# A decoder step's output product and feed-forward start from operands split one program ahead, and the last down products take three inner blocks of a pair, then the fourth

## The chip, the core and the metric

One core of a Trainium2 chip runs the whole program. The metric is the device time of one execution in microseconds (us). The engines are TensorE (PE in the profile; PEld is its weight load), VectorE (DVE), ScalarE (ACT), GpSimd (POOL) and SyncE (SP), which here only issues DMAs.

## What is computed

One inference step of one decoder layer, for a prompt of 1024 positions and 32 sample positions, all in float32. The part that matters here is the end of the layer:

```
gate = sigmoid(proj[..., OFF_MG:OFF_MG + 3 * D_MODEL].reshape(bn, t, 3, D_MODEL))
h = gate[:, :, 0] * (o_a @ wa) + gate[:, :, 1] * (o_b @ wb) + gate[:, :, 2] * (o_c @ wc)
x = x + h @ wo
...
q = rms_norm((rms_norm(x, g_x) @ w_q).reshape(bn, t, M_HEADS, M_HD), q_g)
...
x = x + o @ w_o
h = jnp.square(jax.nn.relu(rms_norm(x, g_f) @ w1))
return x + h @ w2
```

D_MODEL is 1024, the feed-forward's hidden width is 4096, and the attention between runs over 256 memory tokens with 4 heads of 128.

## The kernel before

Activations lie with channels on the 128 partitions: `x`, `h` and the like are 8 blocks (KD = 8) of 128 channels by T = 1056 positions. A product over all positions is made in three chunks (NC3 = 3) of NW = 352 positions. Every operand of the large products is split in two fp32r parts: ScalarE copies it rounded (the high part), VectorE subtracts that from the original (the low part), and TensorE adds high x high, high x low and low x high into one PSUM bank. A product of one 128-column weight block with one chunk is thus 8 x 3 = 24 matmuls.

The program is a row of stages, each a block with one instruction list for each engine. At the end of a block all engines meet in a barrier; within it they wait for each other by semaphores. The order on an engine is the order in which the code is written. Four stages matter here.

`stage_merge` (L2937) goes through 24 units: for each branch and each of 8 output blocks, gate product (TensorE, L2983 to L2985), sigmoid (ScalarE, L3032), branch product (L2994 to L2996), and VectorE's multiply and add into `h` (L3065, L3068). Weight blocks of a unit arrive by SP's DMAs into two buffers in turn.

`stage_merged_query` (L3078) makes x + h @ w_out and then, from the normed x, the memory queries. Its 12 weight blocks (8 of `w_out`, 4 of `w_mq`) go through three raw buffers `mw_raw` (NRAW = 3), loaded by SP; a later one is requested when VectorE has made the low part of the block three ahead (L3103 to L3106). `weight_high` (L3156) and `weight_low` (L3207) split them into `mw_slots`. ScalarE and VectorE start this stage with

```
merged_high(0)                 # ScalarE
weight_high(0)
...
merged_low(0)                  # VectorE
weight_low(0)
```

where `merged_high(c)` and `merged_low(c)` split a third of `h` (8 blocks of 352 positions, 2816 elements in a partition) into `h_h` and `h_l`. TensorE waits for both, then runs chunk 0 of all eight blocks, then chunks 1 and 2. GpSimd brings the thirds of x back from memory.

`stage_mem` (L3454) is the memory attention and its output product. At its end it norms x for the feed-forward, for positions 0 to 383 and 384 to 767 ("the middle"): squares, sums by TensorE, root, inverse, `scaled` (L3895) into `xf_scaled`, then the split into `xf_h` and `xf_l`. SP requests the first three blocks of `w_ff1` into `ff_raw` when the attention's last values are there. The middle is only scaled here and split in the next stage.

`stage_ffn` (L3286) has 64 units, each with one weight block of 128 x 1024 elements. An up unit makes one of 32 hidden blocks (relu, square, high part by ScalarE, low part by VectorE, into a ring of five). A down unit takes four hidden blocks (GB = 4; 8 groups, NG = 8) into two output blocks (z = 0, 1), for three chunks each: 72 matmuls (L3386 to L3388). The PSUM banks go in two sets of three in turn; `bank_free(n)` waits until the set's last content was read. The last group's down units come behind the last up unit. Ahead of its 72 matmuls a down unit waits with `e.wait_ge(s_hl, GB * (g + 1))` for all four hidden blocks. The stage opens with weight block 0's split, TensorE's `chunk(0, 0)`, the sums of squares for positions 768 on, `chunk(1, 0)`, the middle's chunks and then the end's.

Of the kernel before, what the change touches and what calls it, by code (L numbers as in the profile page):

```python
# [28 lines left out]
P = 128  # L29
# [502 lines left out]
def raw_slots(nc, K, ctx, tag, kb, nraw):  # L532

    R = Shared()
    R.nraw, R.at = nraw, nc.sbuf_base
# [2401 lines left out]
def stage_merge(nc, K, h, xh, xl, oh, lows, first):  # L2937
# [6 lines left out]
    with ctx:  # L2944
# [16 lines left out]
        def _(e):  # L2961
            for u in range(NU):
# [8 lines left out]
                e.dma_start(braw[:, u % 2, :, :], K.d[names[br]][0, :, P * m:P * m + P].rearrange("(k p) n -> p k n", p=P)).then_inc(s_bin[u % 2], 16)  # L2971

# [27 lines left out]
        def _(e):  # L3000
# [25 lines left out]
            for u in range(NU):  # L3026
# [10 lines left out]
                if u + 2 < NU:  # L3037
                    gate_high(u + 2)

# [38 lines left out]
def stage_merged_query(nc, K, w, wq, h, hh, hl, x, q, h_at, free_at):  # L3078
# [3 lines left out]
    raw = nc.alloc_sbuf_tensor_at("mw_raw", [P, NRAW, KD, P], F32, offset=free_at)  # L3082
    near = nc.alloc_sbuf_tensor_at("mw_slots", [P, 6, 2, KD, P], F32R, offset=free_at + NRAW * KD * P * 4)
# [4 lines left out]
    with nc.Block() as block:  # L3088
        s_hh, s_hl, s_x = K.sem("mw_merged_high"), K.sem("mw_merged_low"), K.sems("mw_x_in", NC3)
        s_in, s_wh, s_wl = K.sems("mw_weights_in", NRAW), K.sem("mw_weights_high"), K.sem("mw_weights_low")  # L3090
# [26 lines left out]
        def _(e):  # L3117
# [34 lines left out]
        def _(e):  # L3152
# [3 lines left out]
            def weight_high(j):  # L3156
                e.wait_ge(s_in[j % NRAW], 16 * (j // NRAW + 1))
                if j in (6, 7):
                    e.wait_ge(s_hl, NC3)
# [4 lines left out]
            def squares(c):  # L3164
                e.wait_ge(s_out, count(c, KD - 1))
                e.wait_ge(s_hl, NC3)
# [13 lines left out]
            merged_high(0)  # L3180
            weight_high(0)
# [20 lines left out]
        def _(e):  # L3202
# [4 lines left out]
            def weight_low(j):  # L3207
                e.wait_ge(s_wh, j + 1)
# [31 lines left out]
            merged_low(0)  # L3240
            weight_low(0)
            weight_low(1)
# [43 lines left out]
def stage_ffn(nc, K, xh, xl, xl32, x, ahead):  # L3286
# [20 lines left out]
    with ctx:  # L3307
        W = weight_slots(nc, K, ctx, "ff", KD, ahead=ahead)
        hh = ctx.enter_context(nc.sbuf_tensor("ff_hidden_high", [P, RING, T], F32R))
        hl = ctx.enter_context(nc.sbuf_tensor("ff_hidden_low", [P, RING, T], F32R))  # L3310
        act = ctx.enter_context(nc.sbuf_tensor("ff_act", [P, 2, T], F32))
        rstd = ctx.enter_context(nc.sbuf_tensor("ff_rstd", [P, T - LAST], F32))
# [5 lines left out]
        s_mid_h, s_mid_l = K.sem("ff_middle_high"), K.sem("ff_middle_low")  # L3318
# [19 lines left out]
        def _(e):  # L3338
# [12 lines left out]

            e.wait_ge(W.s_lo, 1)
# [7 lines left out]
            e.wait_ge(s_mid_h, 1)  # L3360
            e.wait_ge(s_mid_l, 1)
# [8 lines left out]
            for u, un in list(enumerate(units))[2:]:  # L3370
# [7 lines left out]
                g = un[1]  # L3378
                e.wait_ge(s_hl, GB * (g + 1))
                for z in range(2):  # L3380
                    bank_free(n)
                    for c in range(NC3):
                        o, ns = K.ps[:, 3 * (n % 2) + c, 0:NW], slice(NW * c, NW * c + NW)
                        for k in range(GB):
                            r = (GB * g + k) % RING
                            e.matmul(o, W.hi[:, u % NSPL, 2 * k + z, :], hh[:, r, ns], start=k == 0, stop=False)  # L3386
                            e.matmul(o, W.hi[:, u % NSPL, 2 * k + z, :], hl[:, r, ns], start=False, stop=False)  # L3387
                            mm = e.matmul(o, W.lo[:, u % NSPL, 2 * k + z, :], hh[:, r, ns], start=False, stop=k == GB - 1)  # L3388
                    mm.then_inc(W.s_mm, 1)
# [33 lines left out]
        def _(e):  # L3423
            low_block(e, W, 0)
            low_block(e, W, 1)
            e.wait_ge(s_mid_h, 1)
# [797 lines left out]
```

## Time and profile before

| what | us |
|---|---|
| median of 3 timed runs | 3068.53 (3067.25 to 3068.81) |
| the profiled execution's own time | 3066.65 |
| its span in the trace | 3064.4 |
| TensorE busy with matmuls | 2743.6 (90%) |
| VectorE busy | 1156.6 (38%) |
| ScalarE busy | 795.6 (26%) |

The span is what the trace covers; the execution's time has 2.2 us more around it. TensorE's busy time is the sum over its matmuls, which overlap one another; its clock has two levels, and the profile gives the granted one as a share of the full clock (0.50 or 1.00 in a stretch that lies wholly at one level). A timeline row gives the start, the duration, the engine, the line, the output and the inputs, and in brackets how long the engine had been idle and what ended it.

### The profile page before, as it was taken

The page shows a single profiled execution, that of the slowest core. Times are in us where ns is not written, and L with a number is a line of the kernel's source. Part 1 is how long each engine was busy: PE and PEld are TensorE (multiplying, and loading weights), DVE is VectorE, ACT ScalarE, POOL GpSimd, SP SyncE. Part 2 cuts the span into 40 slices and gives each one's busy share as a digit, 9 for nine tenths or more (in the row PEclk, how much of TensorE's full clock was granted, in tenths as well). Part 3 has the DMA queues.
Part 4 walks back from the last instruction along what each step waited for, and adds up shares of the span by engine and source line. Part 5 has one row for each costly group of instructions (what it writes and reads, how often), then busy time and mean ns, then how long its engine had stood idle before and what let it go on. Part 6 is the DMA issues. An engine that isn't in the chain of part 4 may idle for free. (4 is left out here: it accounts for less than half of the span.)

```text
span 3064.4 us, 49130 instructions
## 1 busy us (share of the span) xinstructions
PE 2743.6 (90%) x21538; PEld 2451.1 (80%) x21538; DVE 1156.6 (38%) x2018; ACT 795.6 (26%) x1243; POOL 163.6 (5%) x215
## 2 busy tenths in 40 slices
PE   5898688886997789988899999899889999999998
PEld 4897588863995555544699999898679999999998
DVE  4433644425053556534222232443443222222222
ACT  3223322211114244432222121221433221222221
POOL 1000222201111000012000000000000000000000
PEclk7999799987998799988899999998999999999999
DMA  4610100004430000047511111401311111111111
GB/s 163 233 50 8 16 3 3 3 4 161 99 85 18 3 1 1 1 142 264 210 52 45 48 46 43 139 10 35 117 28 42 49 42 49 49 48 43 49 42 64
DMA packets 178933, 192.09 MB, mean 63 GB/s; under 512 B 18214, under 2 KB 162897, under 8 KB 173624
## 3 DMA queue, kind: packets, MB, share of 16 engines
q1 hardware_dynamic: 168665, 127.05, 14.0%
q0 software_dynamic: 9888, 61.87, 5.8%
q8 instruction: 170, 2.79, 0.4%
q14 instruction: 42, 0.34, 0.0%
q10 hardware_dynamic: 168, 0.04, 0.0%
HBM read 165.28 MB, written 28.00 MB: 63 GB/s over the span
## 5 line engine op out<-in xcount | busy, mean ns | idle before, releaser
L3386 PE MATMUL ps<-ff_hidden_high,ff_high 128*128 128x352 f32 x768 | 249.1, 324 | 4.8 <-issue 4.8
L3387 PE MATMUL ps<-ff_hidden_low,ff_high 128*128 128x352 f32 x768 | 248.9, 324 | 0.0
L3388 PE MATMUL ps<-ff_hidden_high,ff_low 128*128 128x352 f32 x768 | 248.8, 324 | 0.0
L586 PE MATMUL ps<-xf_h,ff_high 128*128 128x352 f32 x720 | 232.3, 323 | 2.0 <-DVE ff_low L575 2.0
L588 PE MATMUL ps<-xf_h,ff_low 128*128 128x352 f32 x720 | 231.1, 321 | 0.0
L587 PE MATMUL ps<-xf_l,ff_high 128*128 128x352 f32 x720 | 230.9, 321 | 0.0
L2983 PE MATMUL ps<-xn_h,me_gate_w_high 128*128 128x352 f32 x576 | 186.6, 324 | 4.9 <-DVE me_gate_w_low L3044 4.9
L2984 PE MATMUL ps<-xn_l,me_gate_w_high 128*128 128x352 f32 x576 | 185.3, 322 | 0.0
L2985 PE MATMUL ps<-xn_h,me_gate_w_low 128*128 128x352 f32 x576 | 185.2, 322 | 0.0
L3448 DVE TENSOR_TENSOR x<-x,ps 128x1056 f32<-128x1056 f32 x64 | 80.3, 1255 | 235.8 <-PE ps L3388 235.7
L3442 DVE TENSOR_TENSOR ff_hidden_low<-ff_act,ff_hidden_high 128x1056 fp32r<-128x1056 f32 x32 | 40.3, 1258 | 307.7 <-ACT ff_hidden_high L3418 307.7
L3386 PEld LDWEIGHTS ps<-ff_hidden_high,ff_high 128*128 128x128 f32 x768 | 145.3, 189 | 5.1 <-issue 5.1
L3396 ACT ACTIVATE ff_high<-ff_raw 128x1024 fp32r<-128x1024 f32 x64 | 67.4, 1053 | 307.6 <-PE ps L3388 297.8
L3388 PEld LDWEIGHTS ps<-ff_hidden_high,ff_low 128*128 128x128 f32 x768 | 145.5, 189 | 0.0
L3387 PEld LDWEIGHTS ps<-ff_hidden_low,ff_high 128*128 128x128 f32 x768 | 145.3, 189 | 0.0
L2164 PE MATMUL ps<-np_probsT,values_ones 128*65 128x512 f32 x264 | 141.9, 621 | 0.0
L586 PEld LDWEIGHTS ps<-xf_h,ff_high 128*128 128x128 f32 x720 | 135.1, 188 | 2.3 <-DVE ff_low L575 2.3
L587 PEld LDWEIGHTS ps<-xf_l,ff_high 128*128 128x128 f32 x720 | 135.4, 188 | 0.0
L588 PEld LDWEIGHTS ps<-xf_h,ff_low 128*128 128x128 f32 x720 | 135.1, 188 | 0.0
L586 PE MATMUL ps<-xn_h,pj_high 128*128 128x352 f32 x336 | 110.4, 329 | 7.6 <-DVE pj_low L575 7.6
L2983 PEld LDWEIGHTS ps<-xn_h,me_gate_w_high 128*128 128x128 f32 x576 | 108.7, 189 | 5.1 <-issue 5.1
L588 PE MATMUL ps<-xn_h,pj_low 128*128 128x352 f32 x336 | 109.6, 326 | 0.0
(686 smaller groups left out, 6447.9 us busy)
## 6 DMA issues: line engine op xcount, KB each, us to landing
ff_raw<-in_w_ff SPq DMA_DIRECT2D x64, 512.0 KB, 4.0
me_gate_w_raw<-in_w_in SPq DMA_DIRECT2D x23, 512.0 KB, 3.9
pj_raw<-in_w_in SPq DMA_DIRECT2D x13, 512.0 KB, 4.4
xn_high<-xn_h POOLq DMA_DIRECT2D x1, 4224.0 KB, 12.1
xn_low<-xn_l POOLq DMA_DIRECT2D x1, 4224.0 KB, 24.1
xn_h<-xn_high POOLq DMA_DIRECT2D x1, 4224.0 KB, 16.0
xn_l<-xn_low POOLq DMA_DIRECT2D x1, 4224.0 KB, 26.4
xn_h<-xn_high SPq DMA_DIRECT2D x1, 4224.0 KB, 13.0
```

The costliest lines, as they stand in the source:

```text
L586: e.matmul(o, W.hi[:, z, k, :], rh[:, k, n], start=k == ks[0], stop=False)
L587: e.matmul(o, W.hi[:, z, k, :], rl[:, k, n], start=False, stop=False)
L588: mm = e.matmul(o, W.lo[:, z, k, :], rh[:, k, n], start=False, stop=k == ks[-1])
L2164: e.matmul(K.ps[0:65, 2 + z, :], va[:, z, j, g, :], PT[:, G % NPT, :], start=first, stop=j == i).then_inc(s_val, 1)
L2983: e.matmul(K.ps[:, c, 0:NW], wh[:, z, k, :], xh[:, k, chunk(c)], start=k == 0, stop=False)
L2984: e.matmul(K.ps[:, c, 0:NW], wh[:, z, k, :], xl[:, k, chunk(c)], start=False, stop=False)
L2985: mm = e.matmul(K.ps[:, c, 0:NW], wl[:, z, k, :], xh[:, k, chunk(c)], start=False, stop=k == KD - 1)
L3386: e.matmul(o, W.hi[:, u % NSPL, 2 * k + z, :], hh[:, r, ns], start=k == 0, stop=False)
L3387: e.matmul(o, W.hi[:, u % NSPL, 2 * k + z, :], hl[:, r, ns], start=False, stop=False)
L3388: mm = e.matmul(o, W.lo[:, u % NSPL, 2 * k + z, :], hh[:, r, ns], start=False, stop=k == GB - 1)
L3396: e.activation(W.hi[:, u % NSPL, :, :], W.raw[:, u % NRAW, :, :], ACT.Copy).then_inc(W.s_hi, 1)
L3448: e.tensor_tensor(c3(x[:, m, :]), c3(x[:, m, :]), bank(n), ALU.add).then_inc(s_read_down, 1)
```

## The change

The raw weight buffers, the weight slots and the first semaphores of the output product are now made ahead of `stage_merge` and handed to it as `soon`. SP requests w_out's blocks 0, 2 and 1 at the merge's end, each when the merge's buffer under it is free. ScalarE copies seven of the eight high blocks of h's first third there, ahead of the last unit's sigmoids, and block 0's high part behind them. The new function `first_product` makes product 0 of chunk 0 in the order high x high, low weights, low h. Likewise `stage_mem` splits the feed-forward's weight block 0, and its last `scaled(1, 4)` is done at the head of `stage_ffn`, where the middle's split now goes in two halves. To make room, `ff_low`, `ff_hidden_low` and two small tiles lie at other addresses. In the last group, the first down unit (q = 0) runs three of the four hidden blocks for both z, then the fourth for both.

```diff
@@ stage_merge, SyncE
+            for j, gates in ((0, NU - 1), (2, NU - 1), (1, NU)):
+                e.wait_ge(s_g, NC3 * gates)
+                e.dma_start(soon.raw[:, j, :, :], soon.w(j).rearrange("(k p) n -> p k n", p=P)).then_inc(soon.s_in[j], 16)
@@ stage_merge, ScalarE
+                if u == NU - 2:
+                    e.wait_ge(s_h, NC3 * (NU - 1))
+                    e.activation(soon.hh[:, 0:KD - 1, 0:NW], h[:, 0:KD - 1, 0:NW], ACT.Copy)
+            e.wait_ge(soon.s_in[0], 16)
+            e.activation(soon.near[:, 0, 0, :, :], soon.raw[:, 0, :, :], ACT.Copy)
@@ stage_merged_query, SyncE
-            for j in range(NB):
-                if j >= NRAW:
-                    e.wait_ge(s_wl, j - NRAW + 1)
+            for j in range(NRAW, NB):
+                e.wait_ge(s_wl, j - NRAW + 1)
@@ stage_merged_query, TensorE
+            def first_product():
+                for k in range(KD):
+                    if k == KD - 1:
+                        e.wait_ge(s_hh, 1)
+                    e.matmul(bank(0), slot(0)[:, 0, k, :], hh[:, k, chunk(0)], start=k == 0, stop=False)
+                e.wait_ge(s_wl, 1)
+                for k in range(KD):
+                    e.matmul(bank(0), slot(0)[:, 1, k, :], hh[:, k, chunk(0)], start=False, stop=False)
+                for k in range(KD):
+                    if k % 4 == 0:
+                        e.wait_ge(s_hl0, k // 4 + 1)
+                    mm = e.matmul(bank(0), slot(0)[:, 0, k, :], hl[:, k, chunk(0)], start=False, stop=k == KD - 1)
+                mm.then_inc(s_mm, 1)
+
+            first_product()
             for c in range(NC3):
-                e.wait_ge(s_hl, c + 1)
+                if c:
+                    e.wait_ge(s_hl, c)
                 for m in range(KD):
+                    if c == 0 and m == 0:
+                        continue
@@ stage_merged_query, ScalarE
-            merged_high(0)
-            weight_high(0)
+            e.activation(hh[:, KD - 1, chunk(0)], h[:, KD - 1, chunk(0)], ACT.Copy).then_inc(s_hh, 1)
             weight_high(1)
@@ stage_ffn, TensorE
+            def down(u, g, z, n, ks):
...
                 g = un[1]
+                if g == NG - 1 and un[2] == 0:
+                    e.wait_ge(s_hl, GB * (g + 1) - 1)
+                    bank_free(n)
+                    down(u, g, 0, n, range(GB - 1))
+                    bank_free(n + 1)
+                    down(u, g, 1, n + 1, range(GB - 1))
+                    e.wait_ge(s_hl, GB * (g + 1))
+                    down(u, g, 0, n, range(GB - 1, GB)).then_inc(W.s_mm, 1)
+                    down(u, g, 1, n + 1, range(GB - 1, GB)).then_inc(W.s_mm, 1)
+                    n += 2
+                    continue
                 e.wait_ge(s_hl, GB * (g + 1))
@@ stage_ffn, ScalarE
-            weights_high(e, 0)
+            weights_high(e, 1)
             e.activation(xl32[:, :, end], x[:, :, end], ACT.Square).then_inc(s_sq, 1)
-            weights_high(e, 1)
-            e.activation(xh[:, :, middle], xl32[:, :, middle], ACT.Copy).then_inc(s_mid_h, 1)
+            e.activation(xh[:, 0:4, middle], xl32[:, 0:4, middle], ACT.Copy).then_inc(s_mid_h, 1)
+            e.wait_ge(s_mid_n, 1)
+            e.activation(xh[:, 4:8, middle], xl32[:, 4:8, middle], ACT.Copy).then_inc(s_mid_h, 1)
@@ stage_mem, ScalarE, behind its last root
+            high_block(e, ahead, 0, 1)
```

VectorE's lists show the rest of it. At the start of the output product VectorE ran this before; `h_l` is the low part of h, `mw_slots` the weight blocks:

```order
L3201 UNCONDITIONAL_BRANCH
L3205 TENSOR_TENSOR h_l<-h,h_h 128x8x352
L3209 TENSOR_TENSOR mw_slots<-mw_raw,mw_slots 128x1024 x2
L3205 TENSOR_TENSOR h_l<-h,h_h 128x8x352
L3209 TENSOR_TENSOR mw_slots<-mw_raw,mw_slots 128x1024
L3205 TENSOR_TENSOR h_l<-h,h_h 128x8x352
L3209 TENSOR_TENSOR mw_slots<-mw_raw,mw_slots 128x1024
L3215 TENSOR_TENSOR x<-x,ps 128x352
```

And now, at the same place:

```order
L3225 UNCONDITIONAL_BRANCH
L3234 TENSOR_TENSOR mw_slots<-mw_raw,mw_slots 128x1024
L3269 TENSOR_TENSOR h_l<-h,h_h 128x4x352 x2
L3234 TENSOR_TENSOR mw_slots<-mw_raw,mw_slots 128x1024
L3229 TENSOR_TENSOR h_l<-h,h_h 128x8x352
L3234 TENSOR_TENSOR mw_slots<-mw_raw,mw_slots 128x1024
L3229 TENSOR_TENSOR h_l<-h,h_h 128x8x352
L3234 TENSOR_TENSOR mw_slots<-mw_raw,mw_slots 128x1024
L3240 TENSOR_TENSOR x<-x,ps 128x352
```

The low part of weight block 0 has moved ahead of h's first low part, which is made in two halves; the work up to block 3 is the same in sum.

At the end of the memory attention and the start of the feed-forward VectorE ran this before:

```order
L3892 RECIPROCAL mm_rstd<-mm_rstd 128x384
L3884 TENSOR_TENSOR x<-x,ps 128x288
L3897 SCALAR_TENSOR_TENSOR xf_scaled<-x,par,mm_rstd 128x384 x4
L3884 TENSOR_TENSOR x<-x,ps 128x288 x3
L3897 SCALAR_TENSOR_TENSOR xf_scaled<-x,par,mm_rstd 128x384 x4
L3472 UNCONDITIONAL_BRANCH
L3422 UNCONDITIONAL_BRANCH
L575 TENSOR_TENSOR ff_low<-ff_raw,ff_high 128x1024 x2
L3427 TENSOR_TENSOR xf_l<-xf_scaled,xf_h 128x8x384
L3429 TENSOR_SCALAR ff_rstd<-ps 128x288
```

And now:

```order
L3940 RECIPROCAL mm_rstd<-mm_rstd 128x384
L3932 TENSOR_TENSOR x<-x,ps 128x288
L575 TENSOR_TENSOR ff_low<-ff_raw,ff_high 128x1024
L3945 SCALAR_TENSOR_TENSOR xf_scaled<-x,par,mm_rstd 128x384 x4
L3932 TENSOR_TENSOR x<-x,ps 128x288 x3
L3519 UNCONDITIONAL_BRANCH
L3465 UNCONDITIONAL_BRANCH
L3468 SCALAR_TENSOR_TENSOR xf_scaled<-x,par,mm_rstd 128x384 x4
L575 TENSOR_TENSOR ff_low<-ff_raw,ff_high 128x1024
L3474 TENSOR_TENSOR xf_l<-xf_scaled,xf_h 128x4x384 x2
L3476 TENSOR_SCALAR ff_rstd<-ps 128x288
```

One weight split has crossed the stage's end (the two branch rows) upwards, and one scaling downwards.

## Rows read from the trace of the kernel before

**Rows 1.** The page's first part: busy time of each engine, its share, instructions

```profile
PE 2743.6 (90%) x21538; PEld 2451.1 (80%) x21538; DVE 1156.6 (38%) x2018; ACT 795.6 (26%) x1243; POOL 163.6 (5%) x215
```

**Rows 2.** Timeline from the merge to the output product: start, duration (us), engine, line, out<-in

```profile
1947.92 0.47 ACT L3032 ACTIVATE me_gate_sigmoid<-ps 128x352 f32<-128x352 f32 x1 [3.35 <-PE ps L2985]
...
1953.29 0.32 PE L2996 MATMUL ps<-merge_operand_high,me_branch_w_low 128*128 128x352 f32 x1
...
1954.31 0.53 DVE L3068 TENSOR_TENSOR h<-h,me_gate_sigmoid 128x352 f32<-128x352 f32 x1
...
1957.72 3.09 DVE L3205 TENSOR_TENSOR h_l<-h,h_h 128x2816 fp32r<-128x2816 f32 x1 [2.88 <-ACT h_h L3154]
...
1960.73 1.22 DVE L3209 TENSOR_TENSOR mw_slots<-mw_raw,mw_slots 128x1024 fp32r<-128x1024 f32 x1
...
1962.09 0.63 PE L3123 MATMUL ps<-h_h,mw_slots 128*128 128x352 f32 x1 [8.48 <-DVE mw_slots L3209]
...
1974.99 1.22 DVE L3209 TENSOR_TENSOR mw_slots<-mw_raw,mw_slots 128x1024 fp32r<-128x1024 f32 x1
...
1976.26 0.43 PE L3123 MATMUL ps<-h_h,mw_slots 128*128 128x352 f32 x1
```

**Rows 3.** Timeline from the memory attention's end into the feed-forward

```profile
2288.32 1.38 DVE L3884 TENSOR_TENSOR x<-x,ps 128x288 f32<-128x288 f32 x3
...
2288.91 0.29 PE L3599 MATMUL ps<-mm_o_high,mm_w_low 128*128 128x288 f32 x1
...
2289.61 2.20 DVE L3897 SCALAR_TENSOR_TENSOR xf_scaled<-x,par,mm_rstd 128x384 f32<-128x384 f32 x4
...
2294.57 0.66 PE L3347 MATMUL ps<-xf_h,ff_high 128*128 128x352 f32 x1 [5.37 <-DVE ff_low L575]
...
2299.82 4.04 PE L3356 MATMUL ps<-xf_scaled,cst 128*128 128x288 f32 x16
...
2303.89 0.46 DVE L3429 TENSOR_SCALAR ff_rstd<-ps 128x288 f32<-128x288 f32 x1 [1.62 <-PE ps L3356]
...
2312.65 2.56 DVE L3437 TENSOR_TENSOR xf_l<-xf_scaled,xf_h 128x2304 fp32r<-128x2304 f32 x1 [2.23 <-ACT xf_h L3407]
```

**Rows 4.** Timeline around the start of the last group's down units

```profile
2988.20 1.22 DVE L575 TENSOR_TENSOR ff_low<-ff_raw,ff_high 128x1024 fp32r<-128x1024 f32 x1
...
2994.70 0.32 PE L588 MATMUL ps<-xf_h,ff_low 128*128 128x352 f32 x1
...
2995.06 1.05 ACT L3414 ACTIVATE ff_act<-ps 128x1056 f32<-128x1056 f32 x1 [7.12 <-PE ps L588]
...
2998.45 1.26 DVE L3442 TENSOR_TENSOR ff_hidden_low<-ff_act,ff_hidden_high 128x1056 fp32r<-128x1056 f32 x1 [9.04 <-ACT ff_hidden_high L3418]
...
2999.81 0.63 PE L3386 MATMUL ps<-ff_hidden_high,ff_high 128*128 128x352 f32 x1 [4.79 <-issue]
```

**Rows 5.** Table of stretches: length; busy us (instructions) by engine; granted clock, DMA share, GB/s

```profile
1962.10:1966.30 4.20, 4.20 (x14) 4.20 (x15) 0.91 (x1) 2.00 (x2) 0.00 (x0) 0.50 1.10 321
...
2294.60:2297.40 2.80, 2.80 (x10) 2.80 (x11) 1.15 (x1) 2.80 (x3) 0.00 (x0) 0.50 0.50 136
2335.00:2994.00 659.00, 659.00 (x4113) 659.00 (x4112) 171.39 (x142) 150.89 (x144) 0.00 (x0) 1.00 0.15 46
2999.80:3004.00 4.20, 4.19 (x14) 4.20 (x15) 1.05 (x1) 0.00 (x0) 0.00 (x0) 0.50 0.02 4
```

**Rows 6.** Timeline at the boundary from the feed-forward to the store stage

```profile
3047.91 0.32 PE L3388 MATMUL ps<-ff_hidden_high,ff_low 128*128 128x352 f32 x1
...
3048.26 1.25 DVE L3448 TENSOR_TENSOR x<-x,ps 128x1056 f32<-128x1056 f32 x1 [4.50 <-PE ps L3388]
...
3049.84 0.41 PE L4017 MATMUL ps<-cst,x 128*128 128x128 f32 x2 [1.61 <-PEq L3307]
```

**Rows 7.** All DMAs into `mw_raw`, from issue to landing

```profile
DMA to landing us min/median/max: 3.8/6.8/11.7
```

**Rows 8.** Timeline: the feed-forward's third unit, behind a short wait

```profile
2325.36 0.43 PE L586 MATMUL ps<-xf_h,ff_high 128*128 128x352 f32 x1 [2.04 <-DVE ff_low L575]
```

More of the change, by code:

```diff
@@ L2934, in _, with stage_merge @@
             to_channels(1)
[L2937 removed]
+def stage_merge(nc, K, h, xh, xl, oh, lows, first, soon):
     names = ("w_br_a", "w_br_b", "w_br_c")
@@ L3238, in norm_low @@
                 e.tensor_tensor(hl[:, :, chunk(c)], sq[:, :, :], hh[:, :, chunk(c)].bitcast(F32), ALU.subtract).then_inc(s_xl, 1)
-            merged_low(0)
             weight_low(0)
+            e.wait_ge(s_hh, 1)
+            for z in range(2):
+                ks = slice(4 * z, 4 * z + 4)
+                e.tensor_tensor(hl[:, ks, chunk(0)], h[:, ks, chunk(0)], hh[:, ks, chunk(0)].bitcast(F32), ALU.subtract).then_inc(s_hl0, 1)
             weight_low(1)
@@ L3283, in _, with stage_ffn @@
                 take(2, m)
-def stage_ffn(nc, K, xh, xl, xl32, x, ahead):
+def stage_ffn(nc, K, xh, xl, xl32, x, ahead, at):
     GB = 4
@@ L3317, in stage_ffn @@
             "squared", "summed", "mean", "root", "normed", "high", "low"))
-        s_mid_h, s_mid_l = K.sem("ff_middle_high"), K.sem("ff_middle_low")
+        s_mid_n, s_mid_h, s_mid_l = (K.sem("ff_middle_" + x) for x in ("normed", "high", "low"))
         c3 = lambda ap: ap.rearrange("p (c n) -> p c n", c=NC3)
@@ L3350, in chunk @@
                 return mm
+            def down(u, g, z, n, ks):
+                for c in range(NC3):
+                    o, ns = K.ps[:, 3 * (n % 2) + c, 0:NW], slice(NW * c, NW * c + NW)
+                    for k in ks:
+                        r = (GB * g + k) % RING
+                        e.matmul(o, W.hi[:, u % NSPL, 2 * k + z, :], hh[:, r, ns], start=k == 0, stop=False)
+                        e.matmul(o, W.hi[:, u % NSPL, 2 * k + z, :], hl[:, r, ns], start=False, stop=False)
+                        mm = e.matmul(o, W.lo[:, u % NSPL, 2 * k + z, :], hh[:, r, ns], start=False, stop=k == GB - 1)
+                return mm
             e.wait_ge(W.s_lo, 1)
@@ L3381, in _ @@
                     bank_free(n)
[L3382 to L3389, printed above, removed]
+                    down(u, g, z, n, range(GB)).then_inc(W.s_mm, 1)
                     n += 1
@@ L3423, in _ @@
         def _(e):
-            low_block(e, W, 0)
+            for k in range(4, KD):
+                mm = e.scalar_tensor_tensor(xl32[:, k, middle], x[:, k, middle], K.p("norm_ffn_g", k), ahead.rstd[:, 1, :], ALU.mult, ALU.mult)
+            mm.then_inc(s_mid_n, 1)
             low_block(e, W, 1)
-            e.wait_ge(s_mid_h, 1)
-            e.tensor_tensor(xl[:, :, middle], xl32[:, :, middle], xh[:, :, middle].bitcast(F32), ALU.subtract).then_inc(s_mid_l, 1)
+            for z in range(2):
+                ks = slice(4 * z, 4 * z + 4)
+                e.wait_ge(s_mid_h, z + 1)
+                e.tensor_tensor(xl[:, ks, middle], xl32[:, ks, middle], xh[:, ks, middle].bitcast(F32), ALU.subtract).then_inc(s_mid_l, 1)
             e.wait_ge(s_sum, 1)
@@ L3995, in _ @@
                 if m == 4:
+                    low_block(e, ahead, 0)
                     scaled(1, 0)
-            scaled(1, 4)
 def stage_store(nc, K, x):
```

46 lines of the change are left out of this document (28 added, 18 removed).

## Prediction

> **What bounds the kernel now.** I read the page first for the busy shares: TensorE has by far the most work, 2743.6 us of matmuls in a span of 3064.4 us, so the time falls where TensorE idles or runs at its lower clock [rows 1]. The change touches three places, and at each I read the timeline for what TensorE waits for, then the table of stretches for the clock that was granted.
>
> Place A, from the merge of the branches to the output product [rows 2]: TensorE's last merge matmul is issued at 1953.29. VectorE ends the last unit at 1954.31 + 0.53 = 1954.84; behind the block boundary ScalarE makes the high parts of h's first third and of the first weight block, VectorE's two subtractions follow, and TensorE's first matmul comes at 1962.09. It was idle for 8.48 us.
>
> Place B, from the memory attention to the feed-forward [rows 3]: last matmul issued at 2288.91, VectorE still scales until 2289.61 + 2.20 = 2291.81, then ScalarE and VectorE split weight block 0, and TensorE starts at 2294.57, having idled for 5.37 us.
>
> Place C, ahead of the last four down units [rows 4]: the last up matmul is issued at 2994.70, its hidden block is ready (high and low part) at 2998.45 + 1.26 = 2999.71, TensorE goes on at 2999.81. The row calls the 4.79 us of idle time "issue", but the 0.10 us between that subtraction's end and the matmul show what it waited for.
>
> Behind each of these waits the table grants 0.50, the lower of the two levels (1.2 GHz): 14 matmuls in 4.2 us at A and C, 10 in 2.8 us at B [rows 5]. That is 0.30 us for a matmul. At full clock (2.4 GHz) it is 659 us / 4113 = 0.160 us [rows 5]. So each such matmul costs 0.14 us extra: 2.0 us at A and C, 1.4 us at B.
>
> **The change at A.** Blocks 0 to 2 of the output weights are loaded during the merge, block 0's high part and seven of the eight high blocks of h's first third are made there, and the first product takes all high x high, then low weights, then low h. TensorE no longer needs anything from the new block for its first seven matmuls. The boundary costs 0.33 us from VectorE's last end to TensorE's first start, as before the store stage (3048.26 + 1.25 = 3049.51 to 3049.84) [rows 6]. So TensorE starts at 1954.84 + 0.33 = 1955.17.
>
> That is not the gain yet: behind it VectorE has to keep up. Its list up to block 3's low part is now: low block 0 (1.22), half and half of the first h_l (1.62 each, between 1.26 for 1056 elements and 3.09 for 2816), low block 1 (1.22), h_l (3.09), low block 2 (1.22), h_l (3.09), low block 3 (1.22) [rows 2, 4]. Sum 14.30; each of the 7 steps starts 0.08 us before the one ahead has ended (1957.72 + 3.09 against 1960.73), so 13.7 us, and block 3 is ready at 1955.17 + 13.7 = 1968.9. TensorE could be there a little earlier: a product is 24 x 0.16 = 3.84 us, and it meets low block 1 at 1960.7, low block 2 at 1964.8 and low block 3 at 1968.9, with some 0.3 us of waiting at each. Before, block 3 was ready at 1974.99 + 1.22 = 1976.21 and held TensorE up just so, until 1976.26 [rows 2]. **Gain 1976.2 - 1968.9 = 7.3 us.** The clock drops out of this term: even with 14 matmuls at 0.30 us the first product is over at 1955.17 + 4.2 + 1.6 = 1961.0, and three products of 3.84 us bring TensorE to block 3 at 1968.7, still ahead of VectorE.
>
> What was moved, queue by queue: SP issues three of the weight DMAs behind its last merge DMA, where it had nothing left to do; block 1's waits for the last gate product, which ScalarE's sigmoid answers at 1947.92 [rows 2], and has 7.3 us until the boundary, where these DMAs take 3.8 to 11.7 us, median 6.8 [rows 7]; ScalarE asks for it first at about 1955.7 and VectorE at 1959.4. ScalarE's copy of seven blocks (2464 elements, under the 2.55 us of 2816) stands ahead of the last unit's sigmoids. VectorE wants these only when the branch product ends, some 9 us later, so it costs nothing. Blocks 3 to 7 are requested when a low block is done, so all requests come some 7 us earlier together with what needs them. The first of them, block 3, is asked for at 1956.4 with the first third of x in flight: at the median it lands at 1963.2, at the longest landing at 1968.1. The latter makes low block 3 ready at 1968.1 + 1.06 + 1.22 = 1970.4 and leaves 5.8 us. Above, the bound is 7.6 (no wait of 0.3). I take 7.3, since the row itself is of the same chain; bounds 5.8 to 7.6.
>
> **The change at B.** Weight block 0 is split inside the attention stage: ScalarE's copy of 1.06 us lies behind its last root, where it has nothing left in that stage; VectorE's 1.22 us subtraction goes in ahead of the last scaling, and one scaling of 2.20 us goes out to the new stage. VectorE's last addition thus ends at 2288.32 + 1.38 + 1.14 = 2290.84 instead of the scaling at 2291.81, and TensorE starts at 2291.17 [rows 3]. The additions pushed back are not waited for: TensorE's last product needs a bank freed by an addition that stays ahead of the new subtraction.
>
> From there: first chunk 24 x 0.16 = 3.84, then the sums of squares, from whose start to VectorE's mean it is 2303.89 - 2299.82 = 4.07 us [rows 3]. That frees the chain mean, root, inverse, scaling, high, low, from VectorE's 2303.89 to 2312.65 + 2.56 = 2315.21, that is 11.32 us [rows 3]; TensorE reaches it a little early (three more chunks are 11.5 us). So the mean starts at 2291.17 + 3.84 + 4.07 = 2299.08. The moved work must be done by then: scaling to 2293.4, low block 1 to 2294.5, the middle third's copies in two halves behind the square to about 2297.0, their subtractions to 2299.0. Just in time; if late by a few tenths, the gain falls by that. **Gain 2303.89 - 2299.1 = 4.8 us.** At the lower clock it would be 4.8 - 1.4 = 3.4.
>
> Which clock? TensorE's idle time shrinks from 5.37 us to 2291.17 - 2289.20 = 2.0 us. The nearest row is the matmul at 2325.36, with 2.04 us of idle time before it: it takes 0.43 us [rows 8], where the first ones behind the long waits take 0.63, 0.66 and 0.63 [rows 2 to 4]. No fall there. I take the full clock; bounds 3.4 to 4.9.
>
> The Trainium skill, page "TensorE: Matmul & The Clock Gate", section "Part 1: The HAM clock gate", says that the gate is opened by sustained activity and closed by idleness, and that its monitor runs free of the kernel, so that the point varies from run to run. By that rule a gap of this length may still be met by a closing gate in some executions, and the sum at B would be 3.4 instead of 4.8; the 2.04 us gap of this trace didn't meet one.
>
> **The change at C.** The last hidden block isn't needed for three quarters of the first down unit. Two column blocks x 3 chunks x 3 inner blocks x 3 = 54 matmuls now run first, 54 x 0.16 = 8.6 us from 2994.86, over at 3003.5; the hidden block is ready at 2999.71 [rows 4]. Their weights were ready at 2988.20 + 1.22 = 2989.42 [rows 4], and the second bank is free when ScalarE's first activation has read it, about 2996.1, needed at 2999.2. So the wait of 2999.81 - 2994.86 = 4.95 us goes, and with no idle time the fall of the clock too, 2.0 us. What is new: both halves of the unit now end together, 9 matmuls apart. The next unit's first half needs the first half's bank: VectorE's addition starts 0.35 us after the last matmul's issue and takes 1.25 (3047.91 to 3048.26) [rows 6], 1.6 us in all, where TensorE has 10 x 0.16 = 1.6 us of work. A wait of about 0.1 us. **Gain 6.95 - 0.1 = 6.85 us**; bounds 6.4 (the wait 0.5 us) to 7.0.
>
> **Sum.** 7.3 + 4.8 + 6.85 = 18.95 us of the profiled execution: span 3064.4 to 3045.5, its time 3066.65 to 3047.7. The median of the three timed runs, 3068.53, lies 1.9 above that execution, so the forecast is 3068.5 - 18.95 = 3049.6. The bounds add up to 15.6 to 19.5.
>
> **Rivals.** (1) Late weights in the output product. For it: up to 11.7 us to land, and in the shown stretch the DMA share is 1.10 where the first matmuls run [rows 5, 7]. Against: each request moves with its user. The gain at A falls to 5.8, or less when later blocks are late too (2 to 3 us more): 3051 to 3054, 10%. (2) The lower clock at B (with it perhaps 0.3 us of waits): 3051, 12%. (3) The head starts are eaten at the boundary: some engine comes through later than 0.33 us, or a moved split stands in another's way, so that A and B give half and C all: 6 + 6.85 = 13, 3055.5, 5%. (4) Slower. Place: the feed-forward's opening. It now meets TensorE after a short idle with no long wait; if the gate stays at 0.50 there and does not open for a long stretch, each matmul costs 0.14 us. 18.95 / 0.14 = 135 matmuls eat the gain, 180 make the kernel slower by 6 us; 300 of them (the first four up units) cost 42 us: 3092. Against it: behind every long wait the level is back after 10 to 14 matmuls, and 4113 matmuls from 2335 to 2994 run at 1.00 [rows 5]. 3%. (5) The same time within 0.2% (6.1 us, about what a measurement of this kernel can tell from no change) would need two of the three places to fail: 4%.
>
> **How the numbers follow.** The forecast with its bounds has 66%, (1) and (2) together 22, (3) 5, (4) 3, (5) 4. Forecast, (1), (2) and (3) are all faster by over 6.1 us: 93%. Low end: the largest gain from the lowest time shown, 3066.65 - 19.5 = 3047, less 1 us for the spread of runs; high end: to rival (3), 3056.
>
> **What would show it.** A: TensorE's first output matmul 0.3 to 0.4 us behind VectorE's last merge row, low block 3 about 13.7 us behind it. B: under 2.3 us of idle time, granted clock 1.00 in the first chunk, the mean 8 us behind the start. C: no gap ahead of the down units, no stretch at 0.50, a wait of 0.1 us after the 72nd matmul. A first matmul at A later than 1956.5, 0.50 at B, or a gap of over 0.5 us behind C's first unit would prove the terms wrong.

## The result and the profile after

| | before | after |
|---|---|---|
| first comparison, median us (range, executions) | 3068.67 (3067.25 to 3071.55, 4) | 3040.94 (3039.11 to 3043.73, 4) |
| the same two kernels again | 3068.74 (3059.91 to 3079.71, 17) | 3043.53 (3041.49 to 3046.99, 6) |
| ratio after to before, first and again (95% interval) | | 0.9906 [0.9895, 0.9918]; 0.9916 [0.9899, 0.9933] |
| span of the first profiled execution | 3064.4 | 3036.9 |

The change makes the kernel 25 to 28 us faster; 18.95 were forecast, and 3040.94 lies below the range given (3046 to 3056). The direction was right, the size too small by 6 to 9 us.

Place A after the change, timeline (start, duration, engine, line, output and inputs, idle time before):

```profile
1947.85 0.53 DVE L3076 TENSOR_TENSOR h<-h,me_gate_sigmoid 128x352 f32<-128x352 f32 x1
...
1948.70 1.53 PE L3145 MATMUL ps<-h_h,mw_slots 128*128 128x352 f32 x8 [1.55 <-PEq L2944]
1948.70 1.23 DVE L3234 TENSOR_TENSOR mw_slots<-mw_raw,mw_slots 128x1024 fp32r<-128x1024 f32 x1 [0.32 <-PEq L2944]
...
1954.18 0.43 PE L3130 MATMUL ps<-h_h,mw_slots 128*128 128x352 f32 x1 [0.22 <-DVE mw_slots L3234]
...
1958.18 1.06 ACT L3187 ACTIVATE mw_slots<-mw_raw 128x1024 fp32r<-128x1024 f32 x1 [2.22 <-DMA mw_raw<-in_w_out]
...
1961.19 1.22 DVE L3234 TENSOR_TENSOR mw_slots<-mw_raw,mw_slots 128x1024 fp32r<-128x1024 f32 x1
...
1962.46 0.43 PE L3130 MATMUL ps<-h_h,mw_slots 128*128 128x352 f32 x1
```

The 8.48 us of idle time of [rows 2] are 1.55. TensorE starts 0.32 us behind VectorE's last merge row (1948.38); low block 3 is ready at 1962.41, 13.7 us later, and TensorE takes it up at 1962.46. ScalarE does wait for a DMA at 1958.18, but VectorE is busy with h_l until 1961.26 meanwhile.

Place B after, timeline:

```profile
2275.53 1.22 DVE L575 TENSOR_TENSOR ff_low<-ff_raw,ff_high 128x1024 fp32r<-128x1024 f32 x1
...
2278.78 1.18 DVE L3932 TENSOR_TENSOR x<-x,ps 128x288 f32<-128x288 f32 x3
...
2280.27 0.40 PE L3376 MATMUL ps<-xf_h,ff_high 128*128 128x352 f32 x1 [1.75 <-PEq L3519]
...
2284.17 4.04 PE L3395 MATMUL ps<-xf_scaled,cst 128*128 128x288 f32 x16
...
2288.25 0.46 DVE L3476 TENSOR_SCALAR ff_rstd<-ps 128x288 f32<-128x288 f32 x1
```

The idle time ahead of the feed-forward is 1.75 us in place of 5.37 [rows 3], the first matmul takes 0.40 us, not 0.66, and VectorE's mean comes 7.98 us behind it.

Place C after, timeline:

```profile
2974.19 0.32 PE L588 MATMUL ps<-xf_h,ff_low 128*128 128x352 f32 x1
2974.35 0.32 PE L3386 MATMUL ps<-ff_hidden_high,ff_high 128*128 128x352 f32 x1
...
2977.96 1.26 DVE L3489 TENSOR_TENSOR ff_hidden_low<-ff_act,ff_hidden_high 128x1056 fp32r<-128x1056 f32 x1 [9.05 <-ACT ff_hidden_high L3461]
...
2985.68 0.32 PE L3388 MATMUL ps<-ff_hidden_high,ff_low 128*128 128x352 f32 x1
2986.01 0.40 PE L3386 MATMUL ps<-ff_hidden_high,ff_high 128*128 128x352 f32 x1
```

The gap of 4.79 us [rows 4] is gone. The hidden block is ready at 2979.22, while TensorE is still at the three older ones. The new wait for a bank is the step from 2985.68 to 2986.01, 0.33 us in place of 0.16.

Table of stretches after (length; busy us and instructions of PE, PEld, DVE, ACT, POOL; granted clock, DMA share, GB/s): the same 4113 matmuls as [rows 5]'s long stretch, the first 24 feed-forward matmuls (B), the start of the output product (A), and a piece of the last down units (C).

```profile
2319.50:2973.57 654.07, 654.07 (x4113) 654.07 (x4113) 170.95 (x142) 150.82 (x144) 0.00 (x0) 1.00 0.16 47
2280.30:2284.10 3.80, 3.80 (x24) 3.80 (x25) 3.31 (x5) 3.80 (x3) 0.00 (x0) 1.00 0.49 142
1948.70:1953.00 4.30, 3.73 (x20) 3.13 (x20) 4.30 (x4) 4.30 (x4) 0.96 (x1) 1.00 0.44 126
2979.00:2983.00 4.00, 4.00 (x27) 4.00 (x27) 1.35 (x2) 0.00 (x0) 0.00 (x0) 1.00 0.00 0
```

The clock is full at all three places now. The first row is the surprise: 4113 matmuls at full clock in 654.07 us, where [rows 5] has 659.00 for as many, with TensorE busy without a gap in both. No instruction was taken out of this stretch.

### The profile page after: what moved, and what is told of

It is laid out like the page before. It is cut to its first block and busy times, and to the rows that moved or that the text cites. A ratio compares the mean times of both kernels' runs of the same rounds, so it can differ in the third digit from the quotient of the medians.

```text
span 3036.9 us, 49131 instructions
## 1 busy us (share of the span) xinstructions
PE 2730.9 (90%) x21538; PEld 2440.2 (80%) x21538; DVE 1156.6 (38%) x2020; ACT 795.2 (26%) x1245; POOL 163.7 (5%) x215
```

## Where 27.5 us of span went

I cut both spans at the first matmul of each stage.

| stretch | before | after | less |
|---|---|---|---|
| start to the merge's first matmul (none of it changed) | 1539.4 | 1532.8 | 6.6 |
| merge and output product (A) | 583.2 | 576.2 | 7.0 |
| memory attention (its end holds half of B) | 172.0 | 171.4 | 0.6 |
| feed-forward (rest of B, C) | 755.3 | 742.0 | 13.3 |

The three terms I had priced come to 19.0 of it: A 7.0; C 7.0, from the last up matmul to the store stage; and B 5.0, from the memory attention's last matmul to VectorE's mean (14.98 us before, 10.02 after). The rest, some 8.5 us, is 4.9 us in the feed-forward's 4113 matmuls, 6.6 us in stages that the change doesn't touch, and 2.9 us the other way: from its first to its last matmul the memory attention took 166.4 us before and 169.3 after. (That was the first profile's luck and not the change: before profiled again has 169.6 there, and over all 14 profiles two have 166.4 and 166.6 and twelve 169.1 to 170.1.) Two theories had to be tested: that the 4.9 us come from **where the tiles lie** (the change moves five of the feed-forward's to make room: beside ff_low, ff_hidden_low and the small ff_rstd also ff_hidden_high and ff_act, which the description of the change doesn't list), and that the rest is **the lower clock coming at other moments** in each execution, so that two single profiles differ by it whatever the code. The rival to the second was that the change itself shortens the early stages.

## Experiments

### One part alone, and one part undone

Third part alone (the kernel before, with the branch of the change's last diff piece in stage_ffn):

```diff
+                if g == NG - 1 and un[2] == 0:
+                    e.wait_ge(s_hl, GB * (g + 1) - 1)
...
+                    down(u, g, 0, n, range(GB - 1, GB)).then_inc(W.s_mm, 1)
+                    down(u, g, 1, n + 1, range(GB - 1, GB)).then_inc(W.s_mm, 1)
```

> The kernel before with the third part of the change alone (the last group's first down unit takes three hidden blocks for both z, then the fourth). My term C says 6.85 us less than before (6.4 to 7.0): the 4.95 us of idle time ahead of the last down units gone, no stretch at 0.50 behind it, about 0.1 us of new waiting. In the comparison of the two traces this place gave 7.1 us. Rival: the three parts are not independent and this one alone gives less than 6 or more than 8 us. A second reading rides on it: everything ahead of the last group is the code of before, at the addresses of before, so by both theories of the extra 8.6 us (placement of tiles; luck of the clock) the mean step from one matmul to the next in the down units stays at 161.2 to 161.4 ns, but by the luck of the clock the untouched attention stages may come out anywhere between before's and after's length (nsa prompt stage 349.7 to 353.1 us, sample stage 189.1 to 192.8 us).

Measured: 3062.97 us (12 executions) beside 3068.34 for before (25), ratio 0.9981 [0.9973, 0.9990], so 5.4 us less; below the 6.4 to 7.1 by the medians, within their interval. In its profile the gap is gone and no stretch behind it is at 0.50. Its feed-forward takes 750.7 us, where before profiled again takes 756.9: 6.2 us less. How many matmuls run at 0.50 behind the gap isn't fixed: 11 in before again, 14 in [rows 5], 17 in the next kernel and in every other one that has the moved tiles and not this part, so that the part is worth more there.

Third part undone in the changed kernel (diff as above, with the signs turned):

> The changed kernel with the last group's down units as before (the third part undone). By term C it is 6.4 to 7.1 us longer than the changed kernel, that is some 20.5 to 21.3 us shorter than before; the idle stretch of 4.8 us ahead of the last down units and 14 matmuls at 0.50 are back, and the down units' step stays at 158.3 to 160.5 ns. If the step went with the split down unit instead of with the tiles' place, it is back at 161.3 ns and the kernel is 11 to 12 us longer than the changed one.

Measured: 3052.16 us (5 executions), 0.9946 [0.9933, 0.9959], 16.2 below before, where 20.5 to 21.3 were expected: that rested on the 27.7 us of the first comparison. From the changed kernel's 3043.53 it is 8.6 us away. The gap is back, to the digit, and the clock behind it (timeline, then table of stretches, of this kernel):

```profile
2982.02 0.63 PE L3424 MATMUL ps<-ff_hidden_high,ff_high 128*128 128x352 f32 x1 [4.79 <-issue]
```

```profile
2981.10:2985.30 4.20, 3.28 (x11) 3.31 (x12) 1.95 (x2) 0.47 (x1) 0.00 (x0) 0.50 0.01 4
```

Its feed-forward takes 749.1 us where the changed kernel has 742.0: 7.1 for C in place. The 4113 matmuls take 654.07 us here as well, so the shorter steps don't hang on the split down unit.

First part alone (stage_mem, stage_ffn and the feed-forward's tiles as in before; the merge and output product as in after):

> The kernel before with the first part alone (the output product's operands are split in the merge). Term A says 7.3 us less (5.8 to 7.6); the comparison of traces gave 7.1. If the clock's luck upstream is in fact tied to this part (its code stands ahead of nothing that runs before the merge's end, but the three stages in front came out 6.6 us shorter in the changed kernel), the gain is 13 to 14 us, and the prompt and sample attention stages come out at 349.7 and 189.1 us; if it is not tied, they come out as in before (353.1 and 192.8) or mixed, and the median gain stays at 7.

Measured: 3059.89 us (7 executions), 0.9978 [0.9966, 0.9991], 8.5 less by the medians; the interval, 2.8 to 10.4, holds the 7.3. Merge and output product take 575.5 us in this profile against 583.2, which is 7.7. Upstream the prompt stage took 355.1 us and the sample stage 190.7, neither before's pair nor after's: not tied to this part.

Second part alone, with the placement that it needs:

> The kernel before with the second part alone (feed-forward weight block 0 split in the memory attention, one scaling moved behind it), with the placement that it needs. Term B says 4.8 us (3.4 with the lower clock in the first chunk), the placement 4.9: together 8.3 to 9.7 us below before. TensorE's gap ahead of the feed-forward is 2.0 us. By the clock gate's free running this gap, in this other history, may meet a fall: then the first ten or so matmuls take 0.29 us each and B gives 3.4. If the parts are no sum of their own (the rival), the gain is under 5 or over 13 us.

Measured: 3057.43 us (12 executions), 0.9963 [0.9950, 0.9976], 11.3 less, where 8.3 to 9.7 were expected. By the medians the three parts alone, 8.5, 11.3 and 5.4, come to 25.2 us. The opening is that of the changed kernel, to the digit:

```profile
2294.60 0.40 PE L3348 MATMUL ps<-xf_h,ff_high 128*128 128x352 f32 x1 [1.75 <-PEq L3487]
```

### The same kernels again

> The changed kernel as it is, timed and profiled again beside the kernel before. In the runs so far the kernel before ranges over 11.6 us (3062.8 to 3074.4), its median 3068.3; the undone parts give 5.4 (third part alone), 8.5 (first part alone), 1.9 (placement alone) and 16.2 us (all but the third), which don't add up to 27.7. Theory 'parts plus placement': the three parts (7.1, 4.9, 7.1) and the placed tiles (4.9) make 24 us, the rest of the first comparison was the luck of the clock in few runs; the median is 3043 to 3046 (22 to 26 us below before), and the stages that the change doesn't touch come out differently from profile to profile (merge starting anywhere between 1532 and 1540 us). Rival 'the clock is the change's doing': the stages ahead of the merge get shorter in every execution of the changed kernel; the median stays at 27 to 28 us below before, the merge starts at 1532 to 1534 and the time at 0.50 ahead of it is 337 to 340 us again.

> The kernel before as it is, one more profile. By 'luck' the time at 0.50 ahead of the merge lies anywhere between 337 and 351 us (the six profiles so far, in kernels whose code is the same up to there: 351, 337, 342, 350, 340, 338), and the short wait in the feed-forward's third unit, which met no fall of the clock in the first profile (first matmul 0.43 us), may meet one here. By 'the change's doing' it is 350 us again. The down units' step is 161.2, 161.3 and 161.4 ns again by either.

Measured: after 3043.53 us, 25.2 below before's 3068.74; before again 3063.79 in its one execution. The untouched stages, by the table of stretches (prompt attention, then sample attention), first before:

```profile
993.50:1346.60 353.10, 308.99 (x1384) 190.80 (x1385) 191.85 (x650) 135.35 (x249) 0.00 (x0) 0.91 0.01 3
1346.60:1539.40 192.80, 154.30 (x853) 95.53 (x853) 73.70 (x175) 48.29 (x85) 30.02 (x31) 0.84 0.68 247
```

before again:

```profile
993.30:1343.10 349.80, 305.81 (x1385) 189.66 (x1385) 191.70 (x651) 135.33 (x249) 0.00 (x0) 0.92 0.01 3
1343.10:1532.50 189.40, 152.32 (x852) 94.50 (x853) 73.60 (x175) 48.16 (x85) 29.59 (x31) 0.85 0.70 251
```

and after again:

```profile
995.40:1348.20 352.80, 309.23 (x1385) 191.40 (x1386) 191.80 (x651) 135.43 (x249) 0.00 (x0) 0.91 0.01 3
1348.20:1540.50 192.30, 152.71 (x853) 94.51 (x853) 73.60 (x175) 48.18 (x85) 29.58 (x31) 0.84 0.69 247
```

VectorE's and ScalarE's busy times agree to 0.2 us; what differs is the granted clock, 0.91 or 0.92 and 0.84 or 0.85. The short stages belong to before the second time and the long ones to after: the rival falls, and the 6.6 us were the luck of two single executions. Over all 14 profiles the prompt stage ranges from 349.7 to 355.2 us and the sample stage from 188.6 to 196.6, with no order by kernel.

The same holds at a place I had used as evidence. The short wait of [rows 8] in before again, timeline:

```profile
2321.30 0.66 PE L586 MATMUL ps<-xf_h,ff_high 128*128 128x352 f32 x1 [2.04 <-DVE ff_low L575]
```

The same 2.04 us of idle time, but 0.66 us for the matmul, not 0.43: here the clock fell, for 11 matmuls. It fell at this wait in the profiles of before again, of the first and the third part alone and of all three kernels with only tiles moved; that it didn't in the first profile was the exception, one in seven. In those six the opening was dearer as well, 13 matmuls at 0.50 and not 10, as the table of stretches of the first part alone shows:

```profile
2286.30:2290.10 3.80, 3.80 (x13) 3.80 (x14) 1.22 (x1) 3.80 (x3) 0.00 (x0) 0.50 0.49 142
```

With part B the opening is at full clock in all seven profiles, behind 1.75 us of idle time. The third unit's wait is still there, and the clock stayed full in six of the seven (after, first profile):

```profile
2309.72 0.43 PE L586 MATMUL ps<-xf_h,ff_high 128*128 128x352 f32 x1 [2.05 <-DVE ff_low L575]
```

In the seventh, with the hidden tiles on multiples of 128 bytes, it fell six matmuls later, for 12 of them. So this wait (2.04 to 2.09 us) is followed by 0.50 in six of seven executions whose opening was at 0.50, and in one of seven where the opening was not. That the two hang together is what the counts say; why, the runs don't show.

### Where the tiles lie

Addresses of the feed-forward's tiles, in bytes within a partition:

| tile | before | after |
|---|---|---|
| ff_high | 142304 | 142304 |
| ff_low | 150496 | 180192 |
| ff_hidden_high | 158688 | 150496 |
| ff_hidden_low | 179808 | 188384 |
| ff_act | 200928 | 171616 |

All of them (and ff_rstd, which TensorE doesn't read) at after's places, every instruction as before:

```diff
+        W = weight_slots(nc, K, ctx, "ff", KD, ahead=ahead, low_at=at + 50176)
...
+        hl = nc.alloc_sbuf_tensor_at("ff_hidden_low", [P, RING, T], F32R, offset=at + 58368)
```

> The kernel before with every instruction in its place; only the addresses of the feed-forward's tiles are those of the changed kernel (ff_low and ff_hidden_low behind the others, ff_hidden_high and ff_act closer). Theory 'placement': the 4.9 us by which the feed-forward's inside got shorter, unexplained by the three parts, come from where the tiles lie: the mean step from matmul to matmul in the down units falls from 161.2-161.4 to 158.3-160.5 ns and the kernel is 4 to 5.5 us shorter than before. Rival 'order': the tiles' place does nothing, the steps are shorter since something else runs beside them (or the trace of before was an unlucky one): difference below 1 us, step unchanged at 161.3 ns.

Measured: 3066.43 us (11 executions), 1.9 below before, ratio 0.9991 [0.9982, 1.0000]: less than the 4 to 5.5 expected by the median, and the interval holds both 0 and 5. The timing alone doesn't show the effect; the trace is sharper here, since the steps repeat. The stretch of 4113 matmuls, table of stretches:

```profile
2340.82:2994.85 654.03, 654.03 (x4113) 654.03 (x4112) 170.95 (x142) 150.79 (x144) 0.00 (x0) 1.00 0.16 47
```

Then, in the kernel before, only ff_hidden_low, ff_act and ff_rstd were moved, the hidden low tile to where after has it. (This kernel and the three others of this section that were executed once took 3061.33, 3063.66, 3051.63 and 3046.62 us, in their order.)

> The kernel before with only ff_hidden_low and ff_act placed elsewhere (ff_hidden_low where the changed kernel has it, ff_act ahead of it; ff_hidden_high and ff_low, and so all weight tiles, stay). If the shorter step comes from where ff_hidden_low lies, the step behind the high x low matmuls falls from 161.3 to about 158.9 ns and the other two stay (gain 1.8 us in 768); if it comes from ff_low and ff_hidden_high, all three stay at 161.2 to 161.4. One look is enough, since this step came out within 0.1 ns in every profile of one placement.

```profile
2334.71:2988.75 654.04, 654.04 (x4114) 654.04 (x4113) 170.96 (x142) 150.78 (x144) 0.00 (x0) 1.00 0.15 47
```

My expectation was wrong: not one of the three steps fell but all three. Next, a move of 384 bytes in the kernel before (ff_act and ff_rstd, behind it, move along; shortened):

```diff
-        hl = ctx.enter_context(nc.sbuf_tensor("ff_hidden_low", [P, RING, T], F32R))
+        hl = nc.alloc_sbuf_tensor_at("ff_hidden_low", [P, RING, T], F32R, offset=ahead.at + 49792 + 384)
```

> The kernel before with ff_hidden_low (and ff_act and ff_rstd behind it) 384 bytes higher, all else in place. In the run with only ff_hidden_low and ff_act moved all three steps of the down units came out as in the changed kernel (160.5, 159.0, 158.3 ns), the same for each ring slot and chunk within 0.2 ns, though ff_hidden_high lay 8192 bytes away from where the changed kernel has it. The old and the new address of ff_hidden_low differ by 8576 = 8192 + 384 bytes. Theory 'low address bits': only the 384 count; this kernel has the short steps too (160.5, 158.9, 158.3). Rival 'which neighbour': it was ff_act's place or the tiles' order; the steps stay at 161.2, 161.3, 161.4 ns.

```profile
2337.05:2991.09 654.04, 654.04 (x4114) 654.04 (x4113) 170.97 (x142) 150.81 (x144) 0.00 (x0) 1.00 0.15 47
```

Moving the tile by 384 bytes gives the kernel before the shorter steps. And 128 bytes (with ff_rstd behind it) take them from the changed kernel:

```diff
-        hl = nc.alloc_sbuf_tensor_at("ff_hidden_low", [P, RING, T], F32R, offset=at + 58368)
+        hl = nc.alloc_sbuf_tensor_at("ff_hidden_low", [P, RING, T], F32R, offset=at + 58496)
```

> The changed kernel with ff_hidden_low 128 bytes higher. By 'low address bits' the steps of the down units change again, up to between 158.3 and 161.4 ns or below; the change can't be given beforehand, only that at least one of the three means moves by over 0.5 ns, where from profile to profile of one placement they moved by 0.1. By the rival (only order and neighbours count) they stay at 160.5, 158.9, 158.3.

```profile
2326.63:2985.69 659.06, 659.06 (x4114) 659.06 (x4113) 171.37 (x142) 150.84 (x144) 0.00 (x0) 1.00 0.15 46
```

That is before's stretch again, and its feed-forward takes 747.2 us where after has 742.0. The last two look at 256 bytes more, and at all hidden tiles 32 bytes higher:

> The changed kernel with ff_hidden_low 256 bytes higher. So far the down units' steps came out in two patterns over ring slots and chunks and no third: one where ff_hidden_low starts 96 bytes over a multiple of 512 (kernel before; changed kernel + 128 bytes), with means 161.2, 161.3, 161.4 ns, and one where it starts 480 over (changed kernel; before + 384 bytes), with 160.5, 158.9, 158.3. Here it starts 224 over one, which no kernel had. If the address within 512 bytes sets the step, a third pattern appears; if every placement but the two seen is between them, the feed-forward lasts 742 to 747 us and the kernel 3043 to 3048. A shorter step than 158.9 on average (over 0.5 ns, 1.2 us in 2304) would make this the fastest version. The rest of the kernel is that of the changed one, so it also gives a profile more of the stages that nothing touches.

```profile
2329.69:2983.73 654.04, 654.04 (x4114) 654.04 (x4113) 170.99 (x142) 150.80 (x144) 0.00 (x0) 1.00 0.16 47
```

> The changed kernel with ff_hidden_high, ff_act and ff_hidden_low 32 bytes higher, so that every block of both hidden tiles starts at a multiple of 128 bytes (it was 96 over one). If a read that starts inside a 128-byte piece costs an extra one, the moving operand's 1408 bytes are read in fewer pieces and all three steps fall, to 157 ns or below: up to 1.5 ns x 2304 = 3.5 us. If only the distance between the two tiles counts, nothing changes (160.5, 158.9, 158.3).

```profile
2324.11:2980.93 656.82, 656.82 (x4113) 656.82 (x4113) 171.17 (x142) 150.83 (x144) 0.00 (x0) 1.00 0.16 46
```

With 256 bytes more nothing changes: no third pattern, so it isn't the address within 512 bytes, and 3042.49 us, 0.9908 [0.9892, 0.9925], not to be told from the changed kernel. With the tiles on multiples of 128 bytes the steps even out near 160 ns: neither the fall to 157 nor the unchanged steps that were expected. Steps from one matmul's start to the next in the down units, mean by the line of the first (ns, steps of over 0.2 us left out), worked out from all starts in each trace; kernels in one row agree to 0.2 ns:

| placement | high x high | high x low | low x high | 4113 matmuls, us |
|---|---|---|---|---|
| before (also before again, first or third part alone, after + 128 bytes) | 161.2 | 161.3 | 161.4 | 659.1 |
| after (also again, without C, B alone, tiles moved, hidden low moved, + 384, after + 256) | 160.5 | 158.9 | 158.3 | 654.0 |
| hidden tiles on multiples of 128 bytes | 160.0 | 160.0 | 160.0 | 656.8 |

What the slow row's kernels share is that ff_hidden_low lies an odd multiple of 128 bytes from ff_hidden_high (179808 - 158688 = 21120 = 165 x 128); in the fast ones it is a multiple of 256 (188384 - 150496 = 37888 = 148 x 256). In the last row the distance is a multiple of 256 as well, so the distance isn't all of it. And it may not be the distance: ff_hidden_high starts 224 bytes above a multiple of 256 in every kernel but the last, so ff_hidden_low's own start (96 above one in the slow row, 224 in the fast) tells the two rows apart just as well; no run moved ff_hidden_high by 128 bytes alone. In detail, the step depends on the ring slot and the chunk, each of which shifts the address by an odd multiple of 128 bytes (4224 and 1408): from 155.0 to 162.0 ns in the fast placement, from 158.0 to 165.8 in the slow one, and the same within some 0.2 ns in two profiles of the changed kernel. Of the 5 us in the stretch, 4.3 lie in its 2016 down matmuls (161.3 against 159.2 ns on average) and 0.6 to 0.7 in its up matmuls, though these read no hidden tile (159.3 against 159.0). Which part of the chip does this the runs don't show.

The Trainium skill, page "SBUF — State Buffer", section "Operand start alignment", says that a tensor may start at any multiple of its element size, and adds that this is about legality and not about speed. All placements here are legal by it; the stretch of 659.1, 654.0 or 656.8 us is the speed, which that section leaves open.

## Why the prediction was off, point by point

Profiles differ by luck, so I compare groups of them. Memory attention and feed-forward together took 931.6 and 932.2 us with neither B, C nor placement (first part alone, before again; 927.3 in the first profile, the lucky one). With the placement: 927.7 to 927.9 in three. With B on top: 921.2 and 920.9. With C on top: 913.4 to 913.6 in three. Merge and output product: 582.9 us on average in seven without A, 576.0 in seven with it.

| term | forecast | by groups of profiles |
|---|---|---|
| A | 7.3 | 6.9 |
| B | 4.8 | 927.8 - 921.1 = 6.7 |
| C | 6.85 | 921.1 - 913.5 = 7.6 |
| placement | not in the sum | 931.9 - 927.8 = 4.1 |
| sum | 18.95 | 25.3 |

The timed medians say 25.2 and 26.4 (with 256 bytes) in the other comparisons and 27.7 in the first. How the 25.3 are shared out depends on the order: without the placement C alone leaves 925.9, so 6.0 us in place of 7.6, and the changed kernel with ff_hidden_low 128 bytes higher takes 918.6, so that the placement is worth 5.1 there. The 7.6 also hold some 0.4 us of the memory attention's own spread; by the feed-forward alone C is 7.2.

- **A was right**, chain and size: 0.32 us at the boundary (0.33 forecast), 13.7 us to low block 3 (13.7). (One wording of its working is wrong, not its result: from 1961.0 it is two products of 3.84 us, not three, that lead to 1968.7.) Rival 1, late weights, did not come; one copy waited 2.2 us for its DMA under VectorE's cover.
- **B's chain was right**: 1.75 us of idle time (2.0 forecast), the mean 7.98 us behind the start (7.9), full clock. Between the first two profiles its size was too, 5.0 for 4.8. By the groups it was not, 6.7: I took the cost of before from one execution, in which the opening had 10 matmuls at 0.50 and the wait of [rows 8] met no fall of the clock. In the other six profiles without B the opening had 13, and the clock fell behind that wait as well; with B it did so in one of seven. The 0.43 us in [rows 8] also were my evidence that 2 us of idle time are safe. The conclusion held in seven of seven openings with B, but the evidence didn't: with 2.04 to 2.09 us the matmul took 0.66 us in six of the seven profiles without B. The Trainium skill, page "TensorE: Matmul & The Clock Gate", section "Part 1: The HAM clock gate", says that the gate's monitor runs free of the kernel, so that the point of its change varies from run to run; the traces agree, with 0.43 us in one profile of before and 0.66 in the other behind the same 2.04 us. I applied this to the new gap only; it also said that the old rows could be the lucky ones.
- **C was right**: the gap and the fall gone, a new wait of 0.17 us (0.1 forecast), 7.1 us between two single profiles with the moved tiles and 6.2 without them.
- **The step that failed** is the sum itself: it held for "nothing else moves". The change moves the feed-forward's tiles, as the diff and my own description say, and I costed that at nothing without a sentence. It was worth 4.9 to 5.0 us in the 4113 matmuls alone. (The groups give 4.1, since the kernels with moved tiles and neither B nor C had five or six long steps more, 53 of 0.2 to 0.3 us in the stage against 47 and 48.) With it the forecast would have been 3044.7, just below the range; between the first two spans the miss of 8.6 us is these 4.9, the 6.6 of luck upstream, less the 2.9 of luck in the memory attention. A row was there to ask about: 0.160 us for a matmul of [rows 5] was a mean, and in its down units over steps of 158.0 to 165.8 ns that repeat with the ring's five slots.
- **The low end** was the largest gain from the lowest time shown, less 1 us for the spread. The three timed runs lay within 1.6 us; 17 executions of the same kernel on one chip ranged over 19.8 us. Three executions don't show the spread.
- Rivals 2 to 5 didn't come. The feed-forward's opening at 0.50 for long, the slower case, is refuted by all seven openings.

## What to carry to other kernels

A change that moves a tile is a change of speed until the steps of the instructions that read it are compared: look at the mean step of a long undisturbed stretch before and after, since it repeats to 0.1 us in 650, where the times of the kernel before spread over 10 to 20. A clock level read from one profile behind one wait is one draw; price a wait by the same wait in several profiles, and look at the next wait too, since here a clock that hadn't fallen at the first wait mostly didn't fall at the second (one of seven, against six of seven).

## What the runs showed of the hardware that I had not expected

TensorE's step for the same fp32r matmul of 128 x 352 at full clock and with no wait lies between 155.0 and 165.8 ns on average by ring slot and chunk, and where the two moving tiles start changes it: moving ff_hidden_low 128 bytes up costs 5.0 us in 4113 matmuls (0.8%), and 256 bytes nothing. The step also changes for matmuls that don't read the moved tile: all three lines changed when ff_hidden_low was moved (with ff_act and ff_rstd, which TensorE never reads), though two of them read ff_hidden_high only; the step from a low x high matmul to the next high x high, neither of which reads the moved tile, went from 161.4 to 158.3 ns. The granted clock, in stages with the same instructions, differs so much from execution to execution that a stage of 190 us took from 188.6 to 196.6 us.
